# Expert blocks of 32 slots instead of 64 in a one-core encoder block

## The chip, the core and the metric

The kernel runs on one core of one Trainium2 chip. The metric is the time on the device in microseconds, median of several runs. TensorE does the matrix products, VectorE and ScalarE work on their results in PSUM, GpSimd (POOL) issues the indirect DMAs, SyncE (SP) the others. Each has a sequencer of its own; they wait for one another by semaphores.

## The reference

One encoder layer on 512 tokens of 1,024 values, with 16 meta tokens ahead: attention of two kinds, an output projection, and then 32 experts of which each token takes four. The changed part is the experts:

```python
    logits = (xf @ w_router).astype(jnp.float32) + b_router.astype(jnp.float32)
    top_val, top_idx = lax.top_k(logits, TOP_K)
    gates = jax.nn.softmax(top_val, axis=-1)
    ...
        act = clamped_swiglu(xb @ w1[e] + b1[e])
        return act @ w2[e] + b2[e]
    ...
    y = y.reshape(-1, D_).astype(jnp.float32) * buf_g[:, None]
    out = jax.ops.segment_sum(y, buf_tok, num_segments=T)
```

`w1[e]` is 1,024 x 2,048 and `w2[e]` 1,024 x 1,024 in f32, together 12.58 MB an expert. At the end `h` plus the experts' sum is normed and multiplied by `final_norm`; the meta tokens are dropped, so the kernel routes only the 512 others, 2,048 choices in all. By the reference's router on its inputs the experts get 83, 55, 79, 78, 107, 53, 17, 35, 43, 52, 104, 68, 116, 36, 99, 145, 59, 16, 8, 24, 38, 47, 44, 71, 90, 127, 51, 43, 57, 87, 42 and 74 tokens.

## The kernel before

Attention and the output projection run first, up to about 475 us. After the router VectorE makes tables: how many blocks of 64 tokens each expert needs (at least one), in which order the experts come (`order`; an expert's number in it is its place), which place each block has (`ptab`) and at which block each place ends (`btabi`). Experts with more than one block ("heavy") alternate with those of one block, from place 2 on, until one kind is used up. The blocks' number `nb` is in a register, and each engine runs a loop over the most that can be, with an `If` on `nb`.

A block is 64 slots of one expert, held as 128 partitions: the two halves of a token's row lie in partitions s and 64 + s. So `xfd` (the normed tokens) and `acc` (the running sum), both in DRAM, have rows of half a token, 2 KB. For each block g:

- VectorE compares the slot numbers with each token's rank at the expert (`slot_list`, four operations on L965), TensorE turns this into token, part and gate by four short products (`slot_product`, L1284), and VectorE makes the indices (`slot_rows`).
- GpSimd gathers the 128 half rows into `xg` (L446), TensorE turns them by four transposes (`turn_x`, L1278), ScalarE copies them to `xT` (L637).
- TensorE makes the first product (`up`, L1305): 32 f32 products of 512 columns, and four bf16 products for the bias (L1311). The 64 slots are the weight side; the outputs go to partitions 0 to 63 and 64 to 127, two column groups of the array. The trace has two instructions, each with a weight load, for one f32 product.
- VectorE and ScalarE make the clamped SwiGLU of it (`hidden`, L992 to L997, and L642), four operations of VectorE on 512 columns.
- `finish_block`: four transposes of the result (L1340), its copy by ScalarE (L655), the bias (L1347), and the second product (`down`, L1332), 16 f32 products of 512 columns.
- VectorE multiplies it by the gates into `yb` (L1022), and GpSimd adds the rows to `acc` in DRAM (L467). Then it waits for the landing (L471), and VectorE's next L1022 waits for that (`added`).

TensorE runs block g + 1's first product ahead of block g's `finish_block`. The weights of two places lie in SBUF (`w1t`, `w2t`). SP loads those of place p in order, w1 when the last block of place p - 2 has done its first product (`up_done`), w2 when it has done its second (`y_done`). TensorE's program is chosen by the parity of the place, which its sequencer loads from `ptab` (L1317, and L1344 within `finish_block`) and branches on (L1319, L1350). The loop's own lines are L1366 to L1370. L1274, L1301 and L1330 are register operations at the head of `turn_x`, `up` and `down`. L1080, in the projection of the meta tokens' values, is an older piece: four f32 products per step, one for each group of 32 partitions.

After the last add SP loads `final_norm` and the four token tiles of `acc`; ScalarE squares them (L664), takes the root by Ln and Exp, VectorE scales (L1031), and SP writes the output.

## Time and profile before

| | us |
|---|---|
| runs | 1646.02, 1644.37, 1638.24 |
| median | 1644.37 |
| profiled execution, its own time | 1642.16 |
| its span, first to last instruction | 1640.3 |
| TensorE busy (6,908 products) | 1493.2 |
| VectorE, ScalarE, GpSimd busy | 446.9, 266.1, 194.6 |
| DMA moved | 463.71 MB |

The page cuts the span into 40 slices of 41 us; a digit is the busy share in tenths. The chain of waits goes back from the last instruction to what released each. "Idle before" a group is time in which its engine did nothing just ahead of it. "Issue" there means that no wait in the profile explains it; the registers and branches of an engine's sequencer are not counted as busy, but their lines can be asked for (PEldq is TensorE's).

### The profile page before, as it was taken

What the parts mean: (1) busy time and instruction counts of PE and PEld (TensorE: products, weight loads), DVE (VectorE), ACT (ScalarE), POOL (GpSimd) and SP (SyncE); (2) the same over time, 40 slices, a digit from 0 to 9 for tenths busy, and PEclk for the clock granted to TensorE, in tenths of its full rate; (3) what the DMA queues carried; (4) which work ended last, traced back from release to release, by engine and by line L of the source; (5) the groups of instructions that cost most, each with busy time, mean ns of one, the idle gap of its engine ahead of it and who ended that gap; (6) DMA issues with size and microseconds to landing.
All of it is one profiled execution on the core that took longest, in us unless ns stands there. A gap on an engine that the chain in (4) does not pass through costs nothing.

```text
span 1640.3 us, 20605 instructions
## 1 busy us (share of the span) xinstructions
PE 1493.2 (91%) x6908; PEld 633.6 (39%) x6909; DVE 446.9 (27%) x1260; ACT 266.1 (16%) x444; POOL 194.6 (12%) x280
## 2 busy tenths in 40 slices
PE   5999988878957999999999999999999999999782
PEld 3656533355432333333333333333333333333220
DVE  3010122384352222222212222122222222122122
ACT  3001044442111111011101111011110111011012
POOL 6300000000000111111111111111111111111011
PEclk9999999987967999999999999999999999999996
DMA  9310020111645699999999999986999999999994
GB/s 325 98 38 0 16 88 0 46 62 64 261 162 224 240 402 375 405 380 381 398 377 405 382 392 388 372 333 242 402 375 405 382 379 401 376 405 380 405 401 141
DMA packets 95470, 463.71 MB, mean 283 GB/s; under 512 B 7316, under 2 KB 7572, under 8 KB 62676
## 3 DMA queue, kind: packets, MB, share of 16 engines
q1 hardware_dynamic: 84084, 436.90, 66.7%
q0 software_dynamic: 10976, 26.03, 6.4%
q10 hardware_dynamic: 384, 0.44, 0.1%
q8 instruction: 16, 0.26, 0.1%
q14 instruction: 10, 0.08, 0.0%
HBM read 442.86 MB, written 20.48 MB: 282 GB/s over the span
## 4 chain that ended last, share of the span: by engine, by line
PE 83%; DMA 5%; DVE 4%; issue 3%; ACT 2%; SPq 2%; POOL 0%; DVEq 0%; POOLq 0%; ACTq 0%
PE PS L1305 37%; PE PS L1332 19%; DMA sb_arena<-in_w 4%; PE PS L1071 4%; PE PS L1201 3%; PE PS L1077 3%; PE PS L1075 2%; PE PS L1074 2%; PE PS L1340 2%; PE PS L1278 1%; PE PS L1311 1%; SPq L383 1%; PE PS L1097 1%; PE PS L1131 1%; PE PS L1185 1%
## 5 line engine op out<-in xcount | busy, mean ns | idle before, releaser
L1305 PE MATMUL PS<-sb_arena,sb_work 128*64 128x512 f32 x3008 | 661.6, 597 | 17.9 <-DMA sb_arena<-in_w 16.1
L1305 PEld LDWEIGHTS PS<-sb_arena,sb_work 128*64 128x64 f32 x3008 | 223.4, 138 | 447.0 <-issue 421.8
L1332 PE MATMUL PS<-sb_arena,sb_work 128*64 128x512 f32 x1504 | 333.1, 595 | 12.0 <-issue 11.9
L992 DVE TENSOR_SCALAR sb_work<-PS 128x512 f32<-128x512 f32 x47 | 32.5, 692 | 638.7 <-PE PS L1311 638.7
L1332 PEld LDWEIGHTS PS<-sb_arena,sb_work 128*64 128x64 f32 x1504 | 107.3, 137 | 210.4 <-issue 210.4
L655 ACT ACTIVATE sb_work<-PS 128x512 f32<-128x512 f32 x47 | 28.1, 597 | 943.6 <-PE PS L1340 943.6
L467 POOL DMA_INDIRECT accd<-sb_yb,sb_sidc x47 | 75.4, 1604 | 7.3 <-issue 4.0
L1022 DVE TENSOR_SCALAR sb_yb<-PS,sb_gates 128x512 f32<-128x512 f32 x47 | 35.3, 750 | 130.8 <-PE PS L1332 130.8
L965 DVE TENSOR_SCALAR sb_slots<-sb_ca,sb_b,sb_rk 128x128 bf16<-128x128 f32 x204 | 56.9, 371 | 36.4 <-issue 35.6
L653 ACT ACT_TABLE_LOAD x47 | 60.3, 1283 | 0.8
L445 POOL TENSOR_TENSOR sb_sm<-sb_sm 128x1 f32<-128x1 f32 x50 | 9.6, 192 | 415.2 <-DVE sb_gidx L983 414.8
L1201 PE MATMUL PS<-sb_arena 128*128 128x512 f32 x128 | 57.3, 607 | 1.5 <-DVE sb_arena L850 1.5
L1071 PE MATMUL PS<-sb_arena 128*128 128x512 f32 x128 | 57.6, 612 | 0.6 <-DVE sb_work L713 0.6
L1077 PE MATMUL PS<-sb_arena 128*128 128x512 f32 x128 | 55.3, 592 | 0.0
L446 POOL DMA_INDIRECT sb_work<-xfd,sb_gidx x50 | 50.4, 1007 | 8.4 <-issue 2.2
L471 POOL TENSOR_TENSOR sb_sm<-sb_sm 128x1 f32<-128x1 f32 x47 | 8.9, 188 | 340.4 <-DMA accd<-sb_yb,sb_sidc 340.4
L1185 PE MATMUL PS<-sb_arena 128*128 128x128 f32 x112 | 23.7, 374 | 17.4 <-ACT sb_arena L587 15.9
L1075 PE MATMUL PS<-sb_arena 128*128 128x264 f32 x128 | 38.9, 386 | 0.0
L1074 PE MATMUL PS<-sb_arena 128*128 128x264 f32 x128 | 38.9, 386 | 0.0
L1071 PEld LDWEIGHTS PS<-sb_arena 128*128 128x128 f32 x128 | 24.9, 196 | 33.0 <-issue 31.2
L995 DVE TENSOR_TENSOR sb_work<-sb_work,PS 128x512 f32<-128x512 f32 x47 | 32.3, 687 | 18.9 <-ACT PS L642 18.9
L1201 PEld LDWEIGHTS PS<-sb_arena 128*128 128x128 f32 x128 | 24.7, 196 | 31.5 <-issue 29.8
(251 smaller groups left out, 1142.2 us busy)
## 6 DMA issues: line engine op xcount, KB each, us to landing
sb_arena<-in_w SPq DMA_DIRECT2D x192, 2048.0 KB, 21.4
sb_arena<-in_w_in SPq DMA_DIRECT2D x6, 2048.0 KB, 21.3
sb_arena<-in_x SPq DMA_DIRECT2D x8, 512.0 KB, 6.9
sb_arena<-in_w_out SPq DMA_DIRECT2D x2, 2048.0 KB, 10.1
accd<-sb_arena SPq DMA_DIRECT2D x4, 512.0 KB, 7.9
xfd<-sb_arena SPq DMA_DIRECT2D x4, 512.0 KB, 6.0
sb_arena<-accd SPq DMA_DIRECT2D x4, 512.0 KB, 6.5
out<-sb_arena SPq DMA_DIRECT2D x4, 512.0 KB, 2.8
```

The costliest lines, as they stand in the source:

```text
L446: pool.indirect_dma_start(out=xg, out_offset=None, in_=xfd, in_offset=bass.IndirectOffsetOnAxis(ap=gidx[:, 0:1], axis=0)).then_inc(xg_in, 16)
L467: pool.indirect_dma_start(out=acc, out_offset=bass.IndirectOffsetOnAxis(ap=sidc[:, 0:1], axis=0), in_=yb, in_offset=None, compute_op=ALU.a ...
L653: act.preload_act_table(ACT.Sigmoid)
L965: nc.vector.tensor_scalar(slots[:, t, :], ca[:, C_SLOT:C_SLOT + P], b64[:, bass.ds(n, 1)], rk[:, t, bass.ds(e, 1)], ALU.add, ALU.is_equal)\
L1071: last = mm(PS[:, b, :], w[:, k, f * P:(f + 1) * P], nT[:, k, META:NKEY], **io)
L1074: mm(PS[:, b, 0:n], w[:, k, f * P:(f + 1) * P], nT[:, k, 0:n], **io)
L1075: last = mm(PS[:, b + 1, 0:n], w[:, k, f * P:(f + 1) * P], nT[:, k, n:NKEY], **io)
L1077: last = mm(PS[:, b, :], nT[:, k, META + f * P:META + (f + 1) * P], w[:, k, :], **io)
L1185: last = mm(PS[:, 6 + i % 2, 0:P], aTb[i % 2][:, b, :], v[:, b, 512 + hh * P:512 + (hh + 1) * P], start=j == 0, stop=b == 4)
L1201: last = mm(PS[:, u % 4, :], mixT[:, k, t * P:(t + 1) * P], wo[:, n, k, :], start=k == 0, stop=k == KT - 1)
L1305: mm(PS[half(n), 2 * b + part, :], xT[:, k % 4, half(k // 4)], w[:, k, c:c + 512], start=k == 0, stop=False)
L1332: last = mm(PS[half(n), 4, :], actT[:, k % 4, half(k // 4)], w[:, k, n * 512:(n + 1) * 512], start=False, stop=k == KT - 1)
```

## The change

`SLOTS` becomes 32. A block's 32 slots stand as four quarters of a token's row (Q = 4, QD = 256), in partitions s, 32 + s, 64 + s and 96 + s. `xfd` and `acc` have rows of 1 KB. Each product's 32 slots are the weight side, and the outputs go to four column groups: the first product still has 32 f32 products of 512 columns (256 of the gate and 256 of the linear part side by side, so that both lie in one PSUM bank), the second has 32 of 256 columns instead of 16 of 512. Each work on PSUM by VectorE and ScalarE has 256 columns, and there are two transposes where there were four.

`xg`, `xT`, `yb` and the indices have two buffers, `sidc` too. GpSimd issues the gather of block g + 4 ahead of the add of block g, and waits for the add before that only; the lists are made one block earlier. VectorE copies the expert's part of `g6` into `g6c`, so TensorE no longer loads the expert's number; TensorE loads the places of blocks g and g + 1 together at the head of the loop's body (`place_of`). Heavy now means more than two blocks.

The weights' rows are laid out so that a partition takes two neighbouring rows of `w1` (16 KB in one run), or of `w2` (8 KB), where it took single rows before. The final norm has buffers of its own in the freed weight area (`fh`, `fsq`, `fgain`); the gain is loaded when the last first product is done, two of the four tiles are squared by VectorE, and root and scaling go by pairs of tiles.

```diff
-SLOTS = 64
+SLOTS = 32
+Q = P // SLOTS
+QD = D // Q
+THR = T // SLOTS
 MAXBLK = (T * TOPK + NE * (SLOTS - 1)) // SLOTS
-NG = MAXBLK + 5
+NG = MAXBLK + 7
...
-        xfd = nc.dram_tensor("xfd", [2 * T + P, D // 2], F32, kind="Internal").ap()
-        acc = nc.dram_tensor("accd", [2 * T + P, D // 2], F32, kind="Internal").ap()
+        xfd = nc.dram_tensor("xfd", [Q * T + P, QD], F32, kind="Internal").ap()
+        acc = nc.dram_tensor("accd", [Q * T + P, QD], F32, kind="Internal").ap()
...
-        xg = work[:, 0:512]
-        xT = work[:, 512:1024].rearrange("p (j n) -> p j n", j=4)
-        gat = [work[:, 1024:1536], work[:, 1536:2048]]
-        actT = work[:, 2048:2560].rearrange("p (j n) -> p j n", j=4)
+        def turned(o):
+            return work[:, o:o + QD].rearrange("p (j n) -> p j n", j=2)
+        def pairs(rows, j):
+            return rows.rearrange("p (n j) -> p j n", j=2)[:, j, :]
+        xg = [work[:, 0:QD], work[:, QD:2 * QD]]
+        xT = [turned(2 * QD), turned(3 * QD)]
+        gat = [work[:, 4 * QD:5 * QD], work[:, 5 * QD:6 * QD]]
+        actT = turned(6 * QD)
...
-            return I["w1"][e, 2 * c * P:2 * (c + 1) * P, :].rearrange("(k p) n -> p k n", p=P)
+            return I["w1"][e, c * QD:(c + 1) * QD, :].rearrange("(p j) n -> p j n", j=2)
         def w2v(e, c):
-            return I["w2"][e, 4 * c * P:4 * (c + 1) * P, :].rearrange("(k p) n -> p k n", p=P)
+            return I["w2"][e, 2 * c * QD:2 * (c + 1) * QD, :].rearrange("(c p j) n -> p c j n", c=2, j=2)
+        def w2d(par, c):
...
+            sp.wait_ge(up_done, nb)
+            sp.dma_start(fgain, I["final_norm"].to_broadcast([P, D])).then_inc(acc_in, 16)
             sp.wait_ge(y_out, nb * 16)
...
+            def scatter(n, b):
+                pool.wait_ge(scatter_turn, n + 1)
+                pool.wait_ge(y_ready, 2 * n + 2)
+                nc.gpsimd.tensor_tensor(sm[:, 37:38], ones1, ones1, ALU.mult).then_inc(scatter_turn, 1)
+                pool.indirect_dma_start(out=acc, out_offset=bass.IndirectOffsetOnAxis(
+                    ap=sidc[:, b:b + 1], axis=0), in_=yb[b], in_offset=None,
+                    compute_op=ALU.add).then_inc(y_out, 16)
...
+            gather(0, 0)
+            gather(1, 1)
+            for n in (2, 3, 4):
+                pool.wait_ge(xT_done, n - 1)
+                gather(n, n % 2)
...
-            with pool.Fori(0, MAXBLK) as g:
-                with pool.If(g < nb):
-                    pool.wait_ge(xT_done, g + 3)
-                    gather(g + 3)
-                    pool.wait_ge(rows_turn, g + 1)
-                    pool.wait_ge(y_ready, 2 * g + 2)
-                    nc.gpsimd.tensor_tensor(sm[:, 37:38], ones1, ones1, ALU.mult).then_inc(rows_turn, 1)
-                    pool.indirect_dma_start(out=acc, out_offset=bass.IndirectOffsetOnAxis(ap=sidc[:, 0:1], axis=0),
-                                            in_=yb, in_offset=None, compute_op=ALU.add).then_inc(y_out, 16)
-                    pool.wait_ge(added, g + 1)
-                    pool.wait_ge(y_out, g * 16 + 16)
-                    nc.gpsimd.tensor_tensor(sm[:, 21:22], ones1, ones1, ALU.mult).then_inc(added, 1)
...
+            with pool.Fori(0, MAXBLK // 2) as i:
+                for b in range(2):
+                    g = 2 * i + (1 + b)
+                    with pool.If(g < nb):
+                        pool.wait_ge(xT_done, g + 3)
+                        gather(g + 4, 1 - b)
+                        pool.wait_ge(added, g + 1)
+                        pool.wait_ge(y_out, g * 16)
+                        nc.gpsimd.tensor_tensor(sm[:, 21:22], ones1, ones1, ALU.mult).then_inc(added, 1)
...
+            act.preload_act_table_set("natural_log_exp_and_others")
+            for t in (0, 2):
                 act.wait_ge(x_in[t], 48)
-                act.activation(vreg[:, (1 + t) * D:(2 + t) * D], h[:, t, :], ACT.Square,
-                               accum_out=ss[:, t:t + 1]).then_inc(fin_sq, 1)
-            act.wait_ge(fin_sq, TT)
-            rsqrt(ss[:, 0:TT], rinv[:, 0:TT], D, eps6)
+                act.activation(fsq[:, t, :], fh[:, t, :], ACT.Square, accum_out=ss[:, t:t + 1]).then_inc(fin_sq, 1)
+            for t in (0, 2):
+                act.wait_ge(fin_sq, 1 + t // 2)
...
+                nc.vector.tensor_copy(g6c[:, :, :], g6[:, :, bass.ds(e, 1), :].rearrange("p t e c -> p t (e c)"))\
+                    .then_inc(slots_ready, 1)
...
-                gate, lin = PS[:, 2 * b, :], PS[:, 2 * b + 1, :]
+                gate, lin = PS[:, b, 0:QD], PS[:, b, QD:2 * QD]
...
+            def outputs(n, b):
+                dve.wait_ge(y_done, n + 1)
+                dve.wait_ge(added, n + 1)
+                nc.vector.tensor_scalar(yb[b], PS[:, 4, 0:QD], gates[:, bass.ds(n, 1)], None, ALU.mult)\
+                    .then_inc(y_ready, 1)
+                nc.vector.tensor_copy(sidc[:, b:b + 1], sidx[:, bass.ds(n, 1)]).then_inc(y_ready, 1)
...
-                        slot_rows(g + 3)
-                        slot_list(g + 4)
-                        dve.wait_ge(y_done, g + 1)
-                        dve.wait_ge(added, g + 1)
-                        nc.vector.tensor_scalar(yb, PS[:, 4, :], gates[:, bass.ds(g, 1)], None, ALU.mult)\
-                            .then_inc(y_ready, 1)
-                        nc.vector.tensor_copy(sidc[:, :], sidx[:, bass.ds(g, 1)]).then_inc(y_ready, 1)
+                        slot_rows(g + 4, b, i + 2)
+                        slot_list(g + 5)
...
-                for j in range(4):
-                    last = nc.tensor.transpose(PS[:, 7, j * P:(j + 1) * P], xg[:, j * P:(j + 1) * P], ident)
+                for j in range(2):
+                    last = nc.tensor.transpose(PS[:, 7, j * P:(j + 1) * P], pairs(xg[b], j), ident)
...
-                pe.wait_ge(slots_ready, n * 4 + 4)
+            def slot_product(n):
+                pe.wait_ge(slots_ready, n * 5 + 5)
                 for t in range(TT):
-                    last = mm(PS[:, 5, 0:6], slots[:, t, :],
-                              g6[:, t, bass.ds(e, 1), :].rearrange("p e c -> p (e c)"),
-                              start=t == 0, stop=t == TT - 1)
...
+            def place_of(n):
+                return pe.value_load(ptab[0:1, bass.ds(n, 1)], min_val=0, max_val=NE)
...
-                    for part in range(2):
-                        for n in range(2):
-                            c = part * D + n * 512
-                            mm(PS[half(n), 2 * b + part, :], xT[:, k % 4, half(k // 4)], w[:, k, c:c + 512],
-                               start=k == 0, stop=False)
+                    for c in range(Q):
+                        mm(PS[group(c), b, :].rearrange("p (a n) -> p a n", a=2), xT[b][:, k % 2, group(k // 2)],
...
-                    for n in range(2):
-                        c = part * D + n * 512
-                        last = mm(PS[half(n), 2 * b + part, :], selb[:, b, :], ball[:, c:c + 512],
-                                  start=False, stop=True)
+                bias1 = ball[:, 0:2 * D].rearrange("p (a c n) -> p a c n", a=2, c=Q)
...
-                turn_x(g + 2)
-                slot_product(g + 3, expert(g + 3))
-                at_place = pe.value_load(ptab[0:1, bass.ds(g, 1)], min_val=0, max_val=NE - 1)
+                turn_x(g + 2, b, i + 1)
+                slot_product(g + 4)
                 pe.wait_ge(sel_ready, g + 2)
-                for n in range(2):
-                    mm(PS[half(n), 4, :], selb[:, b, :], ball[:, 2 * D + n * 512:2 * D + (n + 1) * 512],
+                for n in range(Q):
...
+                        here, following = place_of(g), place_of(g + 1)
                         with pe.If(g + 1 < nb):
-                            up_of(g + 1, 1 - b)
+                            up_of(g + 1, following, 1 - b)
                         pe.nop()
-                        finish_block(g, b)
+                        finish_block(g, here, b, i)
                     pe.nop()
```

TensorE, from the end of a second product to the next first one (the even places' case). In these rows `MATMUL` stands for the f32 product, TENSOR_LOAD of `sb_ptab` for the load of a place. Before:

```order
L1369 UNCONDITIONAL_BRANCH
L1369 REGISTER_ALU
L1369 COMPARE_AND_BRANCH
L1370 REGISTER_ALU
L1370 COMPARE_AND_BRANCH
L1317 ISA
L1317 TENSOR_LOAD sb_ptab
L1317 ISA x2
L1318 REGISTER_ALU
L1319 REGISTER_ALU [waits xT_ready]
L1319 COMPARE_AND_BRANCH
L1301 ISA
```

After:

```order
L1412 REGISTER_ALU
L1412 COMPARE_AND_BRANCH
L1338 ISA
L1338 TENSOR_LOAD sb_ptab
L1338 ISA x3
L1338 TENSOR_LOAD sb_ptab
L1338 ISA x2
L1414 COMPARE_AND_BRANCH
L1361 REGISTER_ALU
L1362 REGISTER_ALU [waits xT_ready]
L1362 COMPARE_AND_BRANCH
L1348 ISA
```

The way has a second load and its register operations, and one register operation less. TensorE within `finish_block`, from `turn_x` to the lists before:

```order
L1278 MATMUL PS<-sb_ca,sb_work 128x128 [waits xT_ready,xg_in]
L1278 MATMUL PS<-sb_ca,sb_work 128x128 x3
L1290 ISA
L1290 TENSOR_LOAD sb_etab
L1290 ISA x2
L1282 REGISTER_ALU
L1284 ISA [waits slots_ready]
L1284 MATMUL PS<-sb_g,sb_slots 128x6
L1284 ISA
L1284 MATMUL PS<-sb_g,sb_slots 128x6
```

After, from the transposes of the result to the bias of the second product:

```order
L1383 MATMUL PS<-sb_ca,sb_work 128x128 [waits act_ready]
L1383 MATMUL PS<-sb_ca,sb_work 128x128
L1324 ISA
L1326 REGISTER_ALU [waits xg_in0]
L1328 MATMUL PS<-sb_ca,sb_work 128x128 [waits xT_ready]
L1328 MATMUL PS<-sb_ca,sb_work 128x128
L1332 ISA
L1334 MATMUL PS<-sb_g6c,sb_slots 128x6 [waits slots_ready]
L1334 MATMUL PS<-sb_g6c,sb_slots 128x6 x3
L1389 MATMUL PS<-sb_ball,sb_selb 32x256 [waits sel_ready]
L1389 MATMUL PS<-sb_ball,sb_selb 32x256 x3
```

Transposes come in twos, the load of `sb_etab` has gone, and the four short products stand together; the load of `sb_ptab` that followed them before (L1344) has moved to the place above.

## Rows read from the trace of the kernel before

**Rows 1.** The page, forty slices: busy tenths of TensorE, DMA share.

```profile
PE   5999988878957999999999999999999999999782
...
DMA  9310020111645699999999999986999999999994
```

**Rows 2.** Chain that ended last, in time: start us, length us, what.

```profile
504.96 16.80 PE PS L1305 x64
...
547.63 13.73 PE PS L1305 x64
...
570.53 13.73 PE PS L1305 x64
...
1559.08 29.90 DMA sb_arena<-in_w
```

**Rows 3.** Timeline, last block, second product: start us, length us, engine, line.

```profile
1603.84 7.09 PE L1332 MATMUL PS<-sb_arena,sb_work 128*64 128x512 f32 x32
```

**Rows 4.** Groups by line: shapes, count | busy us, mean ns | idle before.

```profile
L992 DVE TENSOR_SCALAR sb_work<-PS 128x512 f32<-128x512 f32 x47 | 32.5, 692 | 638.7 <-PE PS L1311 638.7
...
L625 ACT ACTIVATE sb_arena<-PS 128x1024 f32<-128x1024 f32 x4 | 4.1, 1013 | 5.9 <-PE PS L1227 5.9
```

**Rows 5.** L1080: its group, and its window (us, PE busy, PEld busy, clock, DMA, GB/s).

```profile
L1080 PE MATMUL PS<-sb_arena 128*16 128x128 f32 x128 | 3.9, 273 | 0.0
...
114.29:116.15 1.86, 1.85 (x64) 1.66 (x64) 1.00 0.03 9
```

**Rows 6.** Timeline, one block from the first product's bias to the second.

```profile
1020.30 0.61 PE L1311 MATMUL PS<-sb_ball,sb_selb 128*64 128x512 bf16 x4
...
1020.84 0.66 PE L1340 MATMUL PS<-sb_ca,sb_work 128*128 128x128 f32 x4
...
1021.53 0.60 ACT L655 ACTIVATE sb_work<-PS 128x512 f32<-128x512 f32 x1 [20.14 <-PE PS L1340]
...
1022.55 7.09 PE L1332 MATMUL PS<-sb_arena,sb_work 128*64 128x512 f32 x32 [0.20 <-issue]
```

**Rows 7.** TensorE's sequencer by line, 1006:1029: ns min/median/max, first and last start.

```profile
L1350 PEldq COMPARE_BRANCH  x2: 80/128/177, 1022.3 to 1025.2; - x2
...
L1317 PEldq FUSED_REGOPS  x2: 42/100/157, 1026.3 to 1026.8; - x2
L1317 PEldq SEQ_ASSERT  x1: 18/18/18, 1027.0 to 1027.0; - x1
...
L1301 PEldq FUSED_REGOPS  x1: 88/88/88, 1027.5 to 1027.5; - x1
```

**Rows 8.** The same for a block in 722:730.

```profile
L1369 PEldq ALU_OP  x1: 36/36/36, 726.9 to 726.9; - x1
...
L1301 PEldq FUSED_REGOPS  x1: 86/86/86, 728.5 to 728.5; - x1
```

**Rows 9.** Window of L1332 alone: length, PE, PEld (instructions started), clock, DMA.

```profile
1022.50:1025.20 2.70, 2.65 (x14) 0.97 (x16) 1.00 1.03 414
```

**Rows 10.** The same of L1305, and the sequencer at L1274.

```profile
1006.50:1017.75 11.25, 11.18 (x54) 3.89 (x54) 1.00 1.03 395
...
L1274 PEldq FUSED_REGOPS  x1: 46/46/46, 1017.7 to 1017.7; - x1
```

**Rows 11.** DMA issues: count, median us from issue to landing.

```profile
sb_work<-xfd,sb_gidx POOLq DMA_INDIRECT x50, 6.8
accd<-sb_yb,sb_sidc POOLq DMA_INDIRECT x47, 9.2
```

**Rows 12.** Window: us, PE, PEld, DVE, ACT, POOL busy, clock, DMA share, GB/s.

```profile
1500.00:1520.00 20.00, 18.73 (x98) 6.94 (x96) 5.78 (x17) 2.88 (x4) 2.99 (x4) 1.00 1.02 412
```

**Rows 13.** The same in the attention stage, two pauses of TensorE.

```profile
250.70:252.40 1.70, 0.00 (x0) 0.00 (x0) 1.67 (x2) 1.70 (x2) 0.00 (x0) 1.00 0.00 0
347.90:351.20 3.30, 0.04 (x1) 0.00 (x0) 3.16 (x9) 2.03 (x7) 0.00 (x0) 0.87 0.00 0
```

**Rows 14.** Chain that ended last, the rows loaded back.

```profile
1619.04 7.64 DMA sb_arena<-accd
```

More of the change, by code:

```diff
@@ L216, in build @@
         o += NG // 2
-        nbt = work[0:NE, o:o + 12]
-        i8u = work[:, o + 13:o + 21].bitcast(U32)
-        o += 21
+        nbt = work[0:NE, o:o + 20]
+        nblk = nbt[:, 1 + THR:2 + THR]
+        i8u = work[:, o + 20:o + 28].bitcast(U32)
+        o += 28
         hot = work[0:NE, o:o + NREL]
@@ L438, in _, with gather @@
                 zero(nc.gpsimd.memset(aTb[i][:, 4, :], 0.0))
-            def gather(n):
+            def gather(n, b):
                 if not (isinstance(n, int) and n == 0):
@@ L935, in _ @@
             step(nc.vector.tensor_copy(ee[:, 1:2], place[:, 6:7]))
-            step(nc.vector.tensor_tensor(place[:, 8:9], place[:, 6:7], nbt[:, 9:10], ALU.subtract))
+            step(nc.vector.tensor_tensor(place[:, 8:9], place[:, 6:7], nblk, ALU.subtract))
             step(nc.vector.tensor_scalar(place[:, 9:10], place[:, 7:8], -1.0, None, ALU.add))
@@ L1001, in _ @@
             slot_list(0)
-            slot_rows(0)
+            slot_rows(0, 0, 0)
             slot_list(1)
@@ L1330, in down, with finish_block @@
                         pe.wait_ge(w2_full[par][k // 4], (at_place // 2) * 16 + 16)
[L1331 to L1333 removed]
+                    for n in range(Q):
+                        last = mm(PS[group(n), 4, 0:QD], actT[:, k % 2, group(k // 2)],
+                                  w[:, k, n * QD:(n + 1) * QD], start=False, stop=k == KT - 1)
                 last.then_inc(y_done, 1)
[L1336 removed]
+            def finish_block(g, at_place, b, i):
                 pe.wait_ge(act_ready, g + 1)
[L1339 to L1340 removed]
+                for j in range(2):
+                    last = nc.tensor.transpose(PS[:, 6, j * P:(j + 1) * P], pairs(gat[b], j), ident)
                 last.then_inc(actT_done, 1)
[L1342 to L1344 removed]
+                turn_x(g + 2, b, i + 1)
+                slot_product(g + 4)
                 pe.wait_ge(sel_ready, g + 2)
[L1346 to L1347 removed]
+                for n in range(Q):
+                    mm(PS[group(n), 4, 0:QD], selb[:, b, :], ball[:, 2 * D + n * QD:2 * D + (n + 1) * QD],
                        start=True, stop=False)
```

204 lines of the change are left out of this document (107 added, 97 removed).

## The prediction

> **What bounds the kernel now.** I read the page first: its slices show TensorE at nine tenths and more from 500 to 1,600 us and the DMA engines at nine tenths beside it [rows 1]. Two resources are that close, so neither share decides. The chain of waits does [rows 2]: from 547 us on it is TensorE alone, and it repeats. A block's first product (L1305) takes 13.73 us, its second (L1332) 7.09 [rows 3], and the rest lies between; starts of L1305 lie 22.9 us apart (547.63, 570.53). There are 47 blocks (the count of L992 [rows 4]). Only near the end does the chain go to weights (29.90 us at 1559.08, and a like one before). So the expert stage is bound by TensorE at 22.9 us a block, and by the DMA where places of one block each follow one another.
>
> The stretch starts at 504.96 [rows 2]; the last L1332 starts at 1603.84 and ends near 1610.8. Sum: 16.8 + 46 x 22.9 + 9.3 = 1079.5, against 1105.9 measured; the 26 us left are weights late at the end.
>
> **How many blocks after.** The reference's router on its inputs gives the 32 experts' counts. Cut by 64 they make 47 blocks, which is what the trace has; cut by 32 they make 81, since the last block of an expert stays part empty. So the two sides of the bargain are 47 x 22.9 = 1,076 us against 81 times the new block, which breaks even at 13.3 us.
>
> **The new block, part by part.**
> First product: 32 f32 products of 512 columns as before, each two instructions, now in four column groups. Can four run at once? L1080 of this kernel is just that (f32, 128 rows, four outputs at partitions 0, 32, 64, 96): its 64 instructions of 128 columns took 1.86 us, where one lasts 273 ns [rows 5], that is, four per 109 ns. Four times the columns give 16 rounds of 0.429 = **6.87 us** (half of 13.73). The halved product of L1332 has 64 instructions of 256 columns: 16 x 0.214 and 0.05 for the first load = **3.48**. Bounds: the same width with two at a time gives 13.73 and 6.9; L1080 speaks against that. The Trainium skill, *TensorE: Matmul & The Clock Gate*, Part 3, gives 2.38 times for three column groups, 0.79 each. By that figure alone the two products would be 13.0 us, an estimate, and the kernel some 220 us slower; L1080 says otherwise, at 128 columns.
>
> Bias of the first product: four bf16 products at once instead of two by two. Before 0.54 from its first start to the transposes (1020.30 to 1020.84 [rows 6]); one round of 0.215 less: **0.32**.
>
> Transposes to the second product: 1020.84 to 1022.55, 1.71 us, ends when ScalarE has copied L655 (1021.53 + 0.60 = 1022.13) and TensorE's sequencer has taken its branch (0.41) [rows 6]. Two transposes instead of four end 0.22 earlier. The copy has 256 columns; 512 take 0.60 us there and 1,024 take 1,013 ns (L625 [rows 4]), so 0.8 ns a column, and 0.21 less. **1.28 us**. What TensorE does beside it (two transposes of rows, four short products, bias) fits below.
>
> Second product to the next first one: 0 in the trace, since a L1305 starts in the rhythm of L1332. But that is cover, and the cover goes. Before the next L1305 the sequencer (registers, branches, a load of the block's place) must come by: it leaves L1332 at 1025.2 (second L1350 branch) and enters L1305 at 1027.5 plus 0.09, 2.4 us [rows 7]; in another block 726.9 to 728.6, 1.7 us [rows 8]. It can leave early because TensorE's queue holds what is issued. How much? At 1025.2 all 64 instructions of L1332 (32 weight loads, 32 products) are issued, and 14 and 16 have started [rows 9], so 34 wait; at 1017.7, at L1274, 54 products of L1305 have started [rows 10] of 72 such pairs issued (64, 4 of L1311, 4 of L1340); 36 instructions wait. The queue gave 34 to 36 in both. In L1332 that is 4.3 us of work: ample. In the new second product it is 36 instructions at 27 ns. In rounds of four (8 instructions, and the loads of one round ahead) the last is issued when round 12 of 16 starts, **1.07 us** before the end. The sequencer's way also gets longer: the place of this block and of the next are both loaded there, a second load with its register operations, from 1026.3 to the end of the assertion that starts at 1027.0 in L1317 = 0.75, less one register operation: +0.68. So 2.07 (middle of 1.7 and 2.4) + 0.68 + 0.05 - 1.07 = **1.75 us** of an idle TensorE each block, where now there is none. Bounds 1.35 and 2.1 from the two blocks. The loads that leave the middle of the block (L1290, L1344) were covered and give nothing back. Issue itself is fast enough: of L1080's 128 instructions 92 were issued within its 1.86 us, under 21 ns each, against 27 wanted.
>
> Block: 6.87 + 0.32 + 1.28 + 3.48 + 1.75 = **13.7 us** (13.3 to 14.2). 81 of them are not less than 47 of 22.9.
>
> **Other engines, all under 13.7.** VectorE: its four operations on 512 columns have 256, each under the 692 ns of L992 [rows 4], so under 2.8 us, and with the lists and one copy more about 7. Adds: an add lands 9.2 us after its issue, under a busy DMA [rows 11]; the next waits for it and for 0.6 us of small steps. Rows of 1 KB instead of 2 should land sooner, rows beside 16 KB runs of weights later; 8 to 11, so nothing up to 13.7. Gathers (6.8 us) have two blocks' time with the second buffer: hidden.
> DMA: 30 experts x 12.58 MB after the first two and 21 MB of rows, at 412 GB/s is 968 us [rows 12] (963 to 1,010 by the 414 and 395 of [rows 9, 10]); two weight rows side by side change the length of a run, not the bytes. It is covered as long as TensorE is the bound, and its 968 us are the next floor if it is not.
> Clock: a pause of 1.70 us left it at 1.00 (2.4 GHz); it fell within one of 3.30 (0.87 over it) [rows 13]. The new pauses are of the first kind.
>
> **The sum.** First L1305 at 502 (504.96 less 3, as the second list no longer waits for the first gather); it takes 10 us, part at 0.50 of the clock (16.8 before, 3 over its 13.73). Then 80 x 13.7 = 1,096, last finish 5, so 1,613. Late weights: by the keys of the order the last five places have two blocks each, 27.4 us against 30.5 for an expert's weights, and one-block places follow three-block ones; 15 to 20 us where before there were 26: 1,630. The end: from 1610.8 to 1640.3, 29.5 us. The final gain is loaded before, 1.3 less; the squares go to two engines and the tables are not reloaded (1.28 twice), but the last rows land at 1626.7 (1619.04 + 7.64 [rows 14]) and set the rest: about 2.5 less. 25.7, so 1,656, and 1.9 outside the span (1642.16 to 1640.3). The profiled execution lies 0.1% under the median: **1658 us**, 0.8% slower than 1644.4.
>
> **Rivals.**
> *The queue covers more.* 34 to 36 were counted with two column groups in use. If each group has its own 17 or 18 places, four hold 68 to 72: the sequencer leaves at round 7 of 16, 2.14 us ahead instead of 1.07, and 80 x 1.07 = 86 us go, some 25 of them given back to late weights: **1,597 us**. Against it: the 36 at L1274 stood ahead of products over all 128 columns too (L1340), and were no more. Chance 0.14. The Trainium skill, *TensorE: Matmul & The Clock Gate*, Part 1, gives TensorE a queue 64 deep; by that figure alone, an estimate, the sequencer would leave at round 8 and the sum be some 70 us less. The trace's 36 differ, and no row here shows the new stream.
> *Weights bound it.* If there is no pause at all, DMA decides: first load for place 2 at 537, 968 us, 15 for the last blocks, 27 for the end: **1,550 us**. For it: the DMA's share is already 0.95. Against: TensorE's sum without any pause is 11.95, so it needs all of that. Chance 0.08.
> *It costs more.* The sequencer takes the long way in each block, or the add (wait for the last, 11 us and more beside 16 KB runs) becomes the round: from 14.2 us a block it is slower than now by over 2%; at 14.8, **1,740 us**. Chance 0.12.
> *Not four at once.* At 512 columns the groups pair up: 22.3 us a block, over 2,300 us. L1080 against it. Chance 0.02.
> *The forecast.* Block 13.3 to 14.2: 1,622 to 1,695. Chance 0.64.
>
> **Numbers.** A measurement of this kernel can tell 0.5% from no change, 1,636 to 1,653. Of the forecast's 0.64, about 0.10 lies under, 0.18 within, 0.36 over. Faster: 0.14 + 0.08 + 0.10 = 0.32; same 0.18; slower 0.36 + 0.14 = 0.50. Range for 8 in 10: the lower end takes in the deeper queue, 1,590; the upper 1,715.
>
> **What would show it.** A round of the first product at 0.43 us with four starts, and its share of the chain near 6.9 us; an idle TensorE of 1.4 to 2.1 us ahead of each first product, put down to issue, not to a semaphore; starts of blocks 13.7 apart; DMA share near 0.9. Wrong if that pause is under 1 us (the queue), if the waits name a weight load through the whole stage (the DMA), or if VectorE's output step waits for the add.

## The result: 0.8% slower, and where the time lies now

The changed kernel takes 1655.88 us (median of five runs, 1651.27 to 1660.05) against 1643.18 of the kernel before (now five runs too): ratio 1.0082, 95% interval 1.0059 to 1.0104. The profiled execution took 1651.27 us, its span is 1649.4.

The page of the changed kernel, the slices of TensorE and of the DMA and the two costliest groups of TensorE (shapes, count | busy us, mean ns | idle before), and VectorE's output step:

```profile
span 1649.4 us, 35953 instructions
...
PE   5999988878938888888888888888878788888883
...
DMA  9310110202636999999699969693999999999994
...
L1350 PE MATMUL PS<-sb_arena,sb_work 128*32 128x512 f32 x5184 | 581.9, 598 | 119.8 <-issue 107.0
...
L1375 PE MATMUL PS<-sb_arena,sb_work 128*32 128x256 f32 x5184 | 296.5, 380 | 28.6 <-issue 28.6
...
L1041 DVE TENSOR_SCALAR sb_yb<-PS,sb_gates 128x256 f32<-128x256 f32 x81 | 39.0, 482 | 2.2 <-PE PS L1375 1.1
```

They answer [rows 1]. TensorE has fallen from nine tenths to eight, and the idle time ahead of the first product (L1350, L1305 before) is 119.8 us, 107.0 of it "issue": no semaphore and no transfer ends it. VectorE's output step L1041, the one that would wait for a late add, has 2.2 us of idle time ahead of it in all 81 blocks together, 1.1 of them ended by TensorE's second product and none by an add.

The chain of waits in two blocks (start us, length us, what), which answers [rows 2, 3, 6]:

```profile
1003.39 7.07 PE PS L1350 x64
1010.46 0.22 PE PS L1355 x4
1010.68 0.44 PE PS L1383 x2
...
1011.66 0.45 issue
1012.10 3.66 PE PS L1375 x64
1015.76 0.95 issue
1016.72 7.07 PE PS L1350 x64
...
1024.98 0.30 issue
1025.28 3.66 PE PS L1375 x64
1028.94 1.56 issue
```

A round is 13.33 and 13.78 us here. First product 7.07, second 3.66, 0.45 and 0.30 of issue ahead of the second, 0.95 and 1.56 ahead of the next first one. Over the 76 rounds that no late weight lengthened the mean is 13.68 us, the mean pause 1.35. So 81 blocks at 13.68 us, 1,108 us, stand against 47 at 22.95, 1,079 us.

Where the pause comes from is in TensorE's sequencer. Its window of L1375 (length, PE, PEld, with the instructions started), and its own lines (ns min/median/max, first and last start), which answer [rows 7 to 9]:

```profile
1012.05:1014.30 2.25, 2.20 (x43) 1.40 (x46) 1.00 0.99 402
...
L1412 PEldq ALU_OP  x1: 36/36/36, 1014.3 to 1014.3; - x1
...
L1338 PEldq FUSED_REGOPS  x4: 42/104/157, 1014.5 to 1015.8; - x4
L1338 PEldq TENSOR_LOAD <-sb_ptab x2: 302/310/317, 1014.6 to 1015.4; - x2
L1338 PEldq SEQ_ASSERT  x2: 18/18/18, 1015.2 to 1016.0; - x2
...
L1348 PEldq FUSED_REGOPS  x1: 93/93/93, 1016.6 to 1016.6; - x1
```

At 1014.30 the sequencer is past L1375; 43 products and 46 weight loads have started of 64 and 64, so 39 instructions stand in the queue. They last until 1015.76. The branches, two loads and their register operations take the sequencer until L1348 at 1016.6, and the next product starts at 1016.72. The queue covers 1.46 us of that way, 0.95 are left. In the next block 1.56 are left: its way has two branches more, one of 0.18 us (L1392, ahead of the other half) and the loop's own of 0.21 (L1409). In all 79 blocks that can be read this way 38 or 39 instructions stood in the queue and lasted 1.46 us in the mean, and the way was 2.81.

Two places' weights come late, each behind a place of one block. TensorE in the timeline there:

```profile
1222.05 1.93 PE L1350 MATMUL PS<-sb_arena,sb_work 128*32 128x512 f32 x16 [1.57 <-issue]
...
1224.24 1.92 PE L1350 MATMUL PS<-sb_arena,sb_work 128*32 128x512 f32 x16 [0.27 <-DMA sb_arena<-in_w]
...
1229.62 1.92 PE L1350 MATMUL PS<-sb_arena,sb_work 128*32 128x512 f32 x16 [3.45 <-DMA sb_arena<-in_w]
...
1234.81 3.46 PE L1350 MATMUL PS<-sb_arena,sb_work 128*32 128x512 f32 x16 [3.27 <-DMA sb_arena<-in_w]
```

### The profile page after: what moved, and what is told of

Read it like the earlier page. It is cut to its first block, busy times and chain, and to the rows that moved or that the text cites. A ratio compares the mean times of both kernels' runs of the same rounds, so it can differ in the third digit from the quotient of the medians.

```text
span 1649.4 us, 35953 instructions
## 1 busy us (share of the span) xinstructions
PE 1389.0 (84%) x13214; PEld 672.1 (41%) x13215; DVE 541.1 (33%) x1943; ACT 308.9 (19%) x577; POOL 307.3 (19%) x451
## 4 chain that ended last, share of the span: by engine, by line
PE 78%; issue 9%; DMA 5%; DVE 5%; ACT 2%; SPq 0%; POOL 0%; DVEq 0%; POOLq 0%; ACTq 0%
PE PS L1350 34%; PE PS L1375 17%; DMA sb_arena<-in_w 4%; PE PS L1251 3%; PE PS L1121 3%; PE PS L1127 3%; PE PS L1383 2%; PE PS L1124 2%; PE PS L1125 2%; PE PS L1328 1%; PE PS L1147 1%; PE PS L1355 1%; PE PS L1181 1%; PE PS L1235 1%; PE PS L1389 1%
## 5 line engine op out<-in xcount | busy, mean ns | idle before, releaser
L1350 PE MATMUL PS<-sb_arena,sb_work 128*32 128x512 f32 x5184 | 581.9, 598 | 119.8 <-issue 107.0
L1350 PEld LDWEIGHTS PS<-sb_arena,sb_work 128*32 128x32 f32 x5184 | 193.1, 110 | 472.5 <-issue 424.2
L1375 PE MATMUL PS<-sb_arena,sb_work 128*32 128x256 f32 x5184 | 296.5, 380 | 28.6 <-issue 28.6
L1030 DVE TENSOR_SCALAR sb_work<-PS 128x256 f32<-128x256 f32 x81 | 34.4, 425 | 644.0 <-PE PS L1355 644.0
L1375 PEld LDWEIGHTS PS<-sb_arena,sb_work 128*32 128x32 f32 x5184 | 166.2, 110 | 135.3 <-issue 43.6
L476 POOL DMA_INDIRECT accd<-sb_yb,sb_sidc x81 | 129.9, 1604 | 12.9 <-issue 2.1
L1000 DVE TENSOR_SCALAR sb_slots<-sb_ca,sb_b,sb_rk 128x128 bf16<-128x128 f32 x344 | 96.3, 360 | 66.6 <-issue 65.8
L468 POOL DMA_INDIRECT sb_work<-xfd,sb_gidx x85 | 85.6, 1007 | 14.3 <-issue 5.3
L1383 PEld LDWEIGHTS PS<-sb_ca,sb_work 128*128 128x128 f32 x162 | 25.4, 206 | 52.7 <-issue 52.7
L1033 DVE TENSOR_TENSOR sb_work<-sb_work,PS 128x256 f32<-128x256 f32 x81 | 34.1, 421 | 29.1 <-ACT PS L675 29.0
L1383 PE MATMUL PS<-sb_ca,sb_work 128*128 128x128 f32 x162 | 40.8, 334 | 1.0 <-issue 1.0
L1041 DVE TENSOR_SCALAR sb_yb<-PS,sb_gates 128x256 f32<-128x256 f32 x81 | 39.0, 482 | 2.2 <-PE PS L1375 1.1
L1235 PE MATMUL PS<-sb_arena 128*128 128x128 f32 x112 | 23.8, 375 | 17.3 <-ACT sb_arena L620 16.0
```

What stands on the lines that cost most here:

```text
L468: pool.indirect_dma_start(out=xg[b], out_offset=None, in_=xfd, in_offset=bass.IndirectOffsetOnAxis(ap=gidx[:, b:b + 1], axis=0)).then_inc( ...
L476: pool.indirect_dma_start(out=acc, out_offset=bass.IndirectOffsetOnAxis(ap=sidc[:, b:b + 1], axis=0), in_=yb[b], in_offset=None, compute_o ...
L1000: nc.vector.tensor_scalar(slots[:, t, :].rearrange("p (q s) -> p q s", s=SLOTS), ca[:, C_SLOT:C_SLOT + SLOTS].unsqueeze(1).to_broadcast([P ...
L1350: mm(PS[group(c), b, :].rearrange("p (a n) -> p a n", a=2), xT[b][:, k % 2, group(k // 2)], w[:, k, :, c, :], start=k == 0, stop=False)
L1375: last = mm(PS[group(n), 4, 0:QD], actT[:, k % 2, group(k // 2)], w[:, k, n * QD:(n + 1) * QD], start=False, stop=k == KT - 1)
L1383: last = nc.tensor.transpose(PS[:, 6, j * P:(j + 1) * P], pairs(gat[b], j), ident)
```

## Experiments

### One load more at the head: three_loads

```diff
-                        here, following = place_of(g), place_of(g + 1)
+                        here, following, unused = place_of(g), place_of(g + 1), place_of(g + 2)
```

> One more load of a place (of block g + 2, used by nothing) at the head of TensorE's loop body. Theory, the sequencer's way: TensorE's sequencer leaves a second product about 1.4 us before its end and comes to the next first product 2.4 to 3.1 us later; each load with its register operations and assertion adds 0.75 us, all of it to the idle time. Pauses 2.1 us instead of 1.35, rounds 14.4 instead of 13.7, 80 x 0.75 = 60 us, of which some 7 come back from weights that are less late: profiled execution about 1,704, 1.038 of the kernel before. Rival, the pause is set by something else (the copy of the next block's rows, an order between the column groups): rounds stay at 13.7, 1,651.

Measured: 1743.97 us, ratio 1.0625 (1.0606 to 1.0645). The mechanism holds, the size doesn't: 102 us over before, where 62 were expected. The median pause went from 1.34 to 1.99, 0.65 more where 0.75 was expected: the third load and its register operations take the sequencer 0.76 us, but one register operation of 0.10 (L1361) is gone from the way. And the first product now comes in two lengths. The timeline (TensorE) and the windows of one block:

```profile
781.35 8.77 PE L1350 MATMUL PS<-sb_arena,sb_work 128*32 128x512 f32 x64 [2.40 <-issue]
...
779.00:781.30 2.30, 0.00 (x0) 0.00 (x0) 0.82 (x5) 0.00 (x0) 1.40 (x2) 1.00 1.00 427
781.98:785.38 3.40, 3.40 (x21) 0.91 (x16) 0.00 (x0) 0.00 (x0) 0.00 (x0) 0.50 0.98 406
```

The pause is 2.40 us, with the granted clock still at 1.00 over it; then it stands at 0.50 (1.2 GHz) for 3.4 us, and the first product takes 8.77 instead of 7.07. That happened 27 times between 505 and 1,600 us, behind pauses of 1.99 us and more, and never behind one of 1.87 or less; 24 other pauses of 1.99 to 2.36 left the clock alone, so the length of a pause doesn't settle it. In the changed kernel the longest ordinary pause is 1.78; its clock fell only at the two blocks that waited for weights, behind idle times of 3.27 and 3.00 us, while that of 3.45 in the timeline above left it at 1.00. So 49 of the 78 rounds of three_loads have 14.40 us in the mean, where 14.4 was expected, and the other 29, with those of late weights, have 1.6 more.

### One load less: one_load

```diff
-                        here, following = place_of(g), place_of(g + 1)
+                        following = place_of(g + 1)
...
+                at_place = place_of(g)
                 pe.wait_ge(actT_ready, g + 1)
```

> The place of the block itself is loaded in finish_block again, behind the bias products (as the kernel before did), and only the next block's place at the head of the body. Theory, the sequencer's way: 0.75 us less in each pause (0.6 instead of 1.35), rounds 12.95; 80 x 0.75 = 60 us less, 12 to 20 of it given back because weights come late more often: about 1,606 (1,598 to 1,614), 0.977 of before. Rival, something else sets the pause: 1,651. Rival, the load in the middle is not hidden: the gap between first and second product grows from 1.49 to 2.2 and the time stays 1,651.

Measured: 1611.98 us, 0.9815 (0.9793 to 0.9836). Pauses 0.57 in the mean, rounds 12.91, and the gap between first and second product unchanged (1.55 us, 1.54 in the changed kernel): the load in the middle is hidden. Rounds behind late weights cost 32 us where the changed kernel has 15. All as the theory had it. This load is the one that the change moved from the middle of the block to the head of the body.

### No load at the head: no_load

```diff
-                        here, following = place_of(g), place_of(g + 1)
+                        following = pe.snap(nextp, min_val=0, max_val=NE)
...
+                at_place = place_of(g)
+                pe.reg_mov(nextp, place_of(g + 2))
                 pe.wait_ge(actT_ready, g + 1)
...
+            nextp = pe.alloc_register("nextp")
+            pe.reg_mov(nextp, pe.value_load(ptab[0:1, 1:2], min_val=0, max_val=NE))
             slot_product(0)
```

> Both loads stand in finish_block behind the bias products; the next block's place is kept in a register of TensorE's sequencer from one block to the next. Theory: the way from a second product to the next first one is 1.5 us shorter, the queue covers it, pauses are 0.1 or less, rounds 12.2. From here on the weights decide: 30 places of 12.58 MB and the rows are some 968 us, TensorE's 81 rounds 988, and the two don't fit without gaps, so 50 to 75 us of late weights where there were 15: 1,570 (1,559 to 1,582), 0.955. Rival, TensorE goes on as the bound with pauses of 0.6 and more because branches weigh more than loads: 1,606. Rival, the two loads in the middle take 1.5 us and don't fit into the 3 us in which the sequencer waits there: the gap between the products grows.

Measured: 1588.67 us, 0.968 (0.9663 to 0.9698). What TensorE waits for ahead of the first product between 540 and 1550 us (us in total, times, longest), in the changed kernel, in one_load and in no_load:

```profile
PE PS L1350 <- issue: 97.2, 72, 1.7
...
PE PS L1350 <- DMA sb_arena<-in_w: 11.7, 5, 3.5
```

```profile
PE PS L1350 <- issue: 43.8, 73, 1.0
...
PE PS L1350 <- DMA sb_arena<-in_w: 17.3, 7, 3.5
```

```profile
PE PS L1350 <- DMA sb_arena<-in_w: 39.2, 17, 4.2
...
PE PS L1350 <- issue: 3.2, 12, 0.3
```

The 97.2 us of issue go to 43.8 and to 3.2, and the waits for weights rise from 11.7 to 17.3 and 39.2. The pause is gone (69 of 78 rounds have 12.28 us in the mean), the gap between the products is still 1.55, so both loads are hidden in the middle, and the bound has changed. The other nine rounds hold 55 us more, within the 50 to 75 expected. The profiled execution, 1584.8, is still 15 us over the 1,570: 6 of them are the 0.08 us a round, 3.5 a first product that starts later (504.1), and the rest lies in my sum, which by its own terms gives 1,580 with 62 us of late weights. Behind the longer waits for weights the granted clock falls too: it was at half for 34 us of this stage, in 7 places, against 6.8 us in the changed kernel.

### The branch ahead of the wait: no_load_late_wait

On top of no_load:

```diff
-                pe.wait_ge(actT_ready, g + 1)
                 with pe.If(at_place % 2 == 0):
...
                         pe.wait_ge(w2_full[par][k // 4], (at_place // 2) * 16 + 16)
+                    if k == 0:
+                        pe.wait_ge(actT_ready, g + 1)
```

> As no_load, and TensorE waits for the copied result (actT_ready) at the first product of the second stage instead of ahead of the branch, so that the branch is taken while ScalarE copies. Theory: 0.35 to 0.4 us off each gap between the products (1.49 to 1.1), 30 us of TensorE's time, but weights bound the stage by then: 10 to 15 us of them arrive, 1,558 (1,546 to 1,570), 0.948. If TensorE were still the bound: 1,540.

Measured: 1576.72 us, 0.9603 (0.9587 to 0.9619), 4.0% under the kernel before and the fastest version that computes what the reference does. The gap lost 0.33 us (1.55 to 1.22), rounds are 11.94. Of the 27 us, 12 arrive, as expected; the level was missed by 19 us, since it was counted from the same low sum.

What TensorE waits for in it, and in fast_light, the next experiment:

```profile
PE PS L1350 <- DMA sb_arena<-in_w: 48.9, 21, 5.8
PE PS L1350 <- issue: 2.9, 12, 0.3
```

```profile
PE PS L1350 <- issue: 3.0, 12, 0.3
```

Its window (us, busy us of PE, PEld, DVE, ACT and POOL, clock, DMA share, GB/s), and that of the changed kernel:

```profile
540.00:1500.00 960.00, 910.38 (x10808) 440.40 (x10800) 331.17 (x1348) 168.56 (x300) 241.59 (x374) 0.97 0.99 399
```

```profile
540.00:1500.00 960.00, 831.05 (x9952) 373.06 (x9948) 308.07 (x1242) 154.99 (x276) 222.62 (x345) 1.00 0.91 366
```

A DMA share of 0.99 at 399 GB/s, against 0.91 at 366: the DMA has hardly any time left.

### The same with light weights: fast_light

```diff
-                        sp.dma_start(w1t(par)[:, 2 * c:2 * c + 2, :],
-                                     I["w1"][bass.ds(e, 1), c * QD:(c + 1) * QD, :]
+                        sp.dma_start(w1t(par)[:, 2 * c:2 * c + 2, 0:512],
+                                     I["w1"][bass.ds(e, 1), c * QD:(c + 1) * QD, 0:512]
```

> no_load_late_wait with only 512 of the 2,048 columns of w1 loaded for places 2 to 31 (the output isn't the reference's; all products are made). Theory: what is left between 81 rounds of 11.93 us and the measured stage is weights that come late. Without them 504 + 9 + 80 x 11.93 + 5 = 1,472 for the last product and 26 for the end: 1,498. Rival, TensorE's halved clock behind pauses or the adds are a part of it: 1,530 and more.

Only a quarter of each row of `w1` is loaded for places 2 to 31, so the output isn't the reference's. Measured: 1505.8 us (two runs, 1503.7 and 1507.91), 0.9171 (0.9126 to 0.9216). The waits for weights are gone from the list above (L1350 <- issue: 3.0 is all that is left ahead of the first product), and the mean over all 78 rounds is 11.94 us, that of the undisturbed rounds of no_load_late_wait. So the 71 us between the two kernels are late weights and what follows them; how much of it is the halved clock (65 us at half there, 3.4 here) was not separated. The expected 1,498 was low by 6 us up to the last product (1477.7 instead of 1,472).

### The kernel before with five loads: before_5_loads

```diff
-                at_place = pe.value_load(ptab[0:1, bass.ds(g, 1)], min_val=0, max_val=NE - 1)
+                for _ in range(5):
+                    at_place = pe.value_load(ptab[0:1, bass.ds(g, 1)], min_val=0, max_val=NE - 1)
```

> The kernel before, with the place of a block loaded five times instead of once ahead of each first product. Theory, the cover: TensorE's sequencer leaves the second product of 7.1 us while 34 of its 64 instructions have yet to start, comes to the next first product 1.7 to 2.4 us later and is 1.9 to 2.6 us ahead there; four loads more are 3.0 us, so that a pause of 0.4 to 1.1 us appears where there was none, some 0.8 in the mean, 45 times 0.8 = 36 us, of which late weights give back some 8: about 1,670, 1.017. Rival, loads cost TensorE's time wherever they stand: 46 x 3.0 = 138 us, 1,780. Rival, the queue covers them all: 1,642.

Measured: 1663.34 us, 1.0121 (1.01 to 1.0142). The sequencer of one block (L1318 is the load) and TensorE's waits:

```profile
L1318 PEldq FUSED_REGOPS  x6: 42/146/157, 1011.8 to 1014.9; - x6
L1318 PEldq TENSOR_LOAD <-sb_ptab x5: 297/301/302, 1011.9 to 1014.5; - x5
L1318 PEldq SEQ_ASSERT  x5: 18/18/18, 1012.5 to 1015.1; - x5
...
PE PS L1305 <- issue: 11.9, 28, 0.7
```

Five loads last from 1011.8 to 1015.1, 0.65 each, so the four added ones are 2.6 us and not 3.0. Rounds are 23.45 us in the mean instead of 22.95 (42 of 44, without those of late weights), 22 us in 45 rounds, of which 18 arrive. Of 2.6 us added to each block 0.5 show; 2.1 are covered by the queue, where the theory had 2.2 in the mean. With 0.65 a load it gives 0.4 us and some 1,660. Neither rival fits. The kernel before pays nothing for its one load there because the 34 instructions in its queue last longer, 4.4 us (1025.2 to 1029.6, [rows 6, 9]).

### The kernel before with the branch ahead of the wait: before_late_wait

The edit of no_load_late_wait, in the kernel before.

> The kernel before, with TensorE's wait for the copied result moved behind the branch on the place, as in no_load_late_wait. Theory: the gap between first and second product, 2.08 to 2.27 us, loses the 0.3 to 0.4 us that the branch takes there, 46 times, 14 to 18 us, of which late weights give back some 3: 1,630, 0.992. If the copy by ScalarE alone sets the gap: 1,643.

Measured: 1629.24 us, 0.9924 (0.9896 to 0.9951). Rounds 22.62 instead of 22.95. As expected. This is the other side of the bargain: a fixed cost of 0.33 us a block is worth 15 us with 47 blocks and 27 us of TensorE's time with 81, though of these only 12 arrived in no_load_late_wait, where the weights bound.

### The weights' layout: old_layout, single_rows, fast_single_rows

The first two kernels change the transposes and the weights of places 0 and 1 only (`w1v`, `w2v`); I had overlooked that SP's loop has the layout of the other thirty written out. For the thirty the rows of `w1` and `w2` are multiplied with other elements than the reference's; the work is the same.

```diff
-            return rows.rearrange("p (n j) -> p j n", j=2)[:, j, :]
+            return rows.rearrange("p (j n) -> p j n", j=2)[:, j, :]
...
-            return I["w1"][e, c * QD:(c + 1) * QD, :].rearrange("(p j) n -> p j n", j=2)
+            return I["w1"][e, c * QD:(c + 1) * QD, :].rearrange("(j p) n -> p j n", j=2)
```

> The changed kernel with the weights' rows one by one again (runs of 8 and 4 KB), the transposes adapted. Theory: the bytes are the same and TensorE is the bound, so nothing, 1,651 to 1,656, 1.008 of before (within 0.3%). If long runs were what keeps the weights on time: 10 to 20 us more at the two places where a block waits for its weights. If they hold up gathers and adds: some less.

> The fastest kernel so far (no_load_late_wait, 1,577) with the same old layout. Here late weights are 68 us of the stage, so a DMA that moves them slower shows at once: by the 5.11 us of a 2 MB chunk in runs of 4 KB against 4.96 in runs of 8 KB, 0.15 a chunk x 60 chunks of w2 = 9 us more, and some 5 of w1: 1,590. If the layout is worth nothing: 1,577 within 0.3%.

Measured: 1649.55 (1.0042, 1.0023 to 1.006) and 1575.46 us (0.9584, 0.9564 to 0.9604). They say nothing on the DMA. They show that a transpose over every second column costs: the gap between the products is 1.48 instead of 1.54, rounds 13.61 instead of 13.68, and a weight load of L1383 takes 0.14 us (median) where the changed kernel's takes 0.21.

With SP's loop changed in the same way (`"e (p j) n -> p (e j) n"` to `"e (j p) n -> p (e j) n"`, and so for `w2`), all places have single rows:

> The changed kernel with the weights of all 32 places in single rows again (runs of 8 and 4 KB; the kernel old_layout had moved the first two places alone), the transposes over neighbouring columns instead of every second one. Theory: TensorE is the bound, so the DMA's layout is worth nothing, and the transposes' 0.06 us a round stays as it was in old_layout: 1,649.5, 1.004. If long runs keep weights on time: 10 us and more above that. If long runs hold up gathers or adds: below it.

> no_load_late_wait with all weights in single rows. Late weights are 68 us of its stage, so here the layout must show if it is worth anything: by the 5.11 us that a 2 MB chunk took in runs of 4 KB against 4.96 in runs of 8 KB before, 60 x 0.15 = 9 us more: 1,585. If the layout is worth nothing: 1,575 within 0.3%. If shorter runs let gathers and adds through faster: under 1,570.

Measured: 1654.6 us (1.0073, 1.0044 to 1.0102) and 1582.65 us (0.9642, 0.9605 to 0.9679). DMA queue of the page (packets, MB, share of the engines), of the changed kernel and of single_rows, and the waits for weights in fast_single_rows:

```profile
q1 hardware_dynamic: 51316, 436.63, 64.8%
```

```profile
q1 hardware_dynamic: 84084, 436.63, 66.0%
```

```profile
PE PS L1350 <- DMA sb_arena<-in_w: 59.1, 21, 4.9
```

The same bytes in 1.6 times the packets. Against the kernels with the same transposes it is 5 us slower (1649.55 to 1654.6) and, where weights bound, 7 us (1575.46 to 1582.65; waits 59.1 us). In both pairs no run of the one reaches the other's, though the first pair's ratios overlap. The traces agree: undisturbed rounds are alike in each pair (13.61, and 11.88 to 11.89), and those of late weights hold 19.3 us more than such rounds against 15.5, and 83 against 75. Two rows side by side are thus worth some 5 us to the changed kernel, and its transposes take as much away: together nothing measurable. I had put the layout at nothing, so single_rows, expected at 1,649.5, was missed by 5 us; fast_single_rows was expected at 1,585.

### The gather behind the add: gather_behind

```diff
-                        pool.wait_ge(xT_done, g + 3)
-                        gather(g + 4, 1 - b)
...
                         scatter(g, 1 - b)
+                        pool.wait_ge(xT_done, g + 3)
+                        gather(g + 4, 1 - b)
```

> The changed kernel with the gather of block g + 4 issued behind the add of block g instead of ahead of it. Theory: a gather is needed two rounds (27 us) after its buffer is free and lands in 7, so up to 14 us later is hidden; and the add is issued about 0.3 us sooner, since the GpSimd doesn't come to its wait behind a gather. TensorE's rounds stay at 13.7: same, 1.008. Rival, the order matters: a gather that waits for the second product's output collides with the weights or comes too late for turn_x, rounds grow by up to 1 us, 1,700 and more.

Measured: 1655.9 us, 1.0071 (1.0048 to 1.0095), rounds of 13.68 and pauses of 1.35 as in the changed kernel. The order on the GpSimd is worth nothing here, as expected; the second buffers give the time in which it hides. Buffers were not taken away, so what a single one would cost stays open. Nor were the copy `g6c`, the new bound of "heavy" and the new final norm tested by runs of their own.

## The prediction, step by step

The forecast of 1,658 stands beside 1655.88, and the mechanism is the one it named: four products at once, and a pause that the queue no longer covers. The steps, in us:

| step | forecast | profiled execution |
|---|---|---|
| first product starts | 502 | 500.6 |
| first round | 10 | 10.7 |
| first product to second, start to start | 8.47 | 8.67 |
| second product and pause | 5.23 | 5.01 |
| round | 13.70 | 13.68 |
| late weights | 15 to 20 | 15.2 |
| end, behind the last product | 25.7 | 23.7 |
| own time | 1,658 | 1651.3 |

- **Four at once.** Right: the first product takes 7.07 us in the chain where L1305 took 13.73, the second 3.66 where L1332 took 7.09. The Trainium skill, *TensorE: Matmul & The Clock Gate*, Part 3, has 2.38 times for three column groups; by that figure the two products would take 13 us, an estimate. They take 10.7 by their full lengths, and the measurement decides.
- **First product to second, 0.2 too short.** The mean of the undisturbed blocks, start to start: first product to bias 6.89 (forecast 6.87), bias to transposes 0.37 (0.32), transposes to second product 1.40 (1.28). The last holds two errors. ScalarE's copy starts 0.54 us behind the first transpose where my terms give 0.47; in old_layout, whose transposes read neighbouring columns, it is 0.47. And behind the copy comes the branch. The copy in the timeline and the branch of TensorE's sequencer, in one block:

```profile
1011.15 0.38 ACT L688 ACTIVATE sb_work<-PS 128x256 f32<-128x256 f32 x1 [11.46 <-PE PS L1383]
...
L1392 PEldq COMPARE_BRANCH  x1: 230/230/230, 1011.7 to 1011.7; - x1
```

The copy was sized right and ends at 1011.53, but the product starts at 1012.10, 0.57 us later, where I had 0.41. It depends on the place: with an even one the branch takes 0.08 us and the product starts 0.42 behind the copy, with an odd one the branch takes 0.23 and it is 0.57. The kernel before has the same two values; I had read one block of it, with an even place. no_load_late_wait shows that 0.33 us of the gap needn't be there.
- **Second product and pause, 0.2 too long.** By its full length the second product takes 3.66, not 3.48, and the pause is 1.35 in the mean, not 1.75 (0.92 to 1.78, so it begins below my bounds). The way is right, 2.81 in the mean; my terms make 2.80 of it (2.07 + 0.68 + 0.05), which with a cover of 1.07 is 1.73 and not 1.75. The cover is what was mis-sized. It is 1.46: 0.18 of the difference is the end of the last products, and 0.21 is that the sequencer leaves earlier, 2.20 us behind the product's start and not 2.41, with 38 or 39 instructions in the queue where I took 36. This error and the one above nearly cancel in the round, 13.68 for 13.70, which is luck. The rival with 68 to 72 places is ruled out by the same count. The Trainium skill, *TensorE: Matmul & The Clock Gate*, Part 1, gives 64; no block of the changed kernel shows more than 39.
- **The sequencer's way.** Right, and shown by changing it three ways: with three, two, one and no load at the head the pauses are 2.0, 1.35, 0.6 and none. A load is 0.65 to 0.77.
- **Weights.** Right in the changed kernel. But the 26 us that I put to late weights in the kernel before hold some 5 that are not: its first round takes 19.6 us, not 16.8, and its mean round 22.95, not 22.9. In the versions without a pause they bound the stage, as that rival said, but at 1,577 and not 1,550: it reckoned with 412 GB/s, and the DMA engines, busy throughout, moved 399; the 968 us are 1,000 at that rate.
- **The add.** It never was the round: VectorE's output step has 2.2 us of idle time ahead of it over the whole stage.
- **The end, 2 us too long.** The last add, the load of the rows behind it and the last square, in the timeline:

```profile
1626.85 1.60 POOL L476 DMA_INDIRECT accd<-sb_yb,sb_sidc  x1
...
1630.72 1.76 SPq L419 DMA_DIRECT2D sb_arena<-accd  x4
...
1638.20 1.23 DVE L1074 SCALAR_TENSOR_TENSOR sb_arena<-sb_arena 128x1024 f32<-128x1024 f32 x1 [1.36 <-DMA sb_arena<-accd]
```

The square waits for the last rows, which are back at 1638.2, 12.5 us behind the last product (1625.7). Before it was 15.8 (1610.9 to the 1626.7 of [rows 14]). I had left that part unchanged. What comes behind it takes 11.2 us (to 1649.4) where my sum had 9.9.

The sum for the profiled execution was 6.6 us too high: 1.4 at the start, 1.6 over the rounds, 2 at the weights, 2 at the end, less 0.7. The start is scatter: in gather_behind, with the same beginning, the first product starts some 2 us later. The median of the runs lies 4.6 us, 0.3%, above the profiled one; I had named 0.1% and not added it. So the nearness of 1,658 to 1655.88 is partly chance.

Where the gain went is then one move: with the block's own place still loaded in the middle (one_load) the same change would have been 1.9% faster, and it is the move of that load to the head that makes it 0.8% slower.

## What to carry to other kernels

A block has a price that its size does not change: here the sequencer's way between two loops of products, 2.4 to 3.2 us. It costs nothing as long as the queue's 34 to 39 instructions last longer. That cover is counted in instructions: the old second product was 64 of them in 7.09 us, and 34 lasted 4.4 us; the new one is 128 in 3.66 us, and 39 last 1.46. So when a tile is made smaller, work out the way and the cover first, and take loads of scalars off the head of a body into a place where the sequencer waits anyway. Here that turns a change that costs 0.8% into one that gives 3.2% (no_load); with the wait behind the branch it is 4.0%, of which the wait alone gives the kernel before 0.8%.

## What the runs showed of the hardware

- TensorE's clock: between 505 and 1,600 us of three_loads idle times of 1.87 us and less left it at 2.4 GHz; behind 27 of those of 1.99 and more it was at 1.2 GHz for 3.4 us, behind 24 it was not. (At 1713.7 us, in the last block, it fell behind one of 1.73 and one of 0.49.) So a load that adds 0.65 us to the pause made the kernel 88 us slower than the changed one, 1.1 us a round.
- A scalar load with its register operations and assertion takes 0.65 us where its address is already there (the five of before_5_loads), and about 0.77 where a register operation works it out first (the two of the changed kernel). A branch of TensorE's sequencer took 0.07 to 0.09 us or 0.18 to 0.23, by the side that it takes.
- Two transposes of the same 256 columns cost TensorE 0.06 to 0.07 us a block more when they take every second column (the gap 1.54 for 1.48, the round 13.68 for 13.61).
- Packets of 16 and 8 KB instead of 8 and 4 KB were worth 7 us in 1,580 where the DMA is the bound (1575.46 to 1582.65), and some 5 where TensorE is (1649.55 to 1654.6).
